# The last layer normalization of a decoder layer in one VectorE pass, its shift as a product in PSUM

## What is computed

```python
def layer_norm(x, g, b):
    xf = x.astype(F32)
    mu = jnp.mean(xf, -1, keepdims=True)
    var = jnp.mean(jnp.square(xf - mu), -1, keepdims=True)
    return ((xf - mu) * lax.rsqrt(var + LN_EPS) * g.astype(F32) + b.astype(F32)).astype(x.dtype)
...
    h = layer_norm(DN_ALPHA * x + mixed, ln1_g, ln1_b)
    f, fbuf = conv_ffn(h, ffn_buf, ffn_w_up, ffn_conv_w, ffn_w_down)
    y = layer_norm(DN_ALPHA * h + f, ln2_g, ln2_b)
```

## Time and profile before

| | us |
|---|---|
| median of 3 runs | 2952.71 |
| lowest, highest | 2946.45, 2958.77 |
| span of the profiled execution | 2947.1 |

### The profile page before, as it was taken

One profiled execution on the slowest core, in us unless ns is written; L12 is line 12 of the kernel. 1 busy time (PEld: TensorE's weight loads), 2 busy tenths in 40 slices (PEclk: granted clock), 3 DMA queues, 4 the chain that ended last, 5 costly groups with the idle time before them and its releaser, 6 DMA issues.

```text
span 2947.1 us, 55566 instructions
## 1 busy us (share of the span) xinstructions
PE 2788.9 (95%) x22685; PEld 2676.0 (91%) x22685; DVE 2278.0 (77%) x3537; ACT 1384.8 (47%) x2371; POOL 359.2 (12%) x332
## 2 busy tenths in 40 slices
PE   8999999999989969999889999999999999999996
PEld 8999999988888658889889999999999999999996
DVE  6656877877657777755688888888888888878898
ACT  4434545545646544522264444444444453434344
POOL 0010000013370315223330000000000000000002
PEclk9999999999989989999999999999999999999998
DMA  7564444448722884563344444444343464434343
GB/s 221 179 206 107 117 119 128 113 150 286 275 82 105 343 247 117 148 175 92 90 157 136 119 126 117 137 115 132 111 141 111 137 194 163 153 112 155 114 124 118
DMA packets 521474, 440.14 MB, mean 149 GB/s; under 512 B 36264, under 2 KB 476767, under 8 KB 515147
## 3 DMA queue, kind: packets, MB, share of 16 engines
q1 hardware_dynamic: 456662, 300.70, 35.6%
q0 software_dynamic: 20288, 82.91, 7.6%
q10 hardware_dynamic: 44272, 52.98, 5.3%
HBM read 378.31 MB, written 66.55 MB: 151 GB/s over the span
## 4 chain that ended last, share of the span: by engine, by line
PE 49%; DVE 5%; issue 1%; ACT 1%; POOL 1%; DMA 1%; DVEq 0%; ACTq 0%; POOLq 0%
PE i L3363 42%; PE i L140 7%; DVE f_half L3869 1%; DMA x_blocks<-s_blk 1%; POOL x_blocks L3311 1%; DVE x_blocks L3907 1%; DVE h_rows L3902 0%; DVE y_rows L4000 0%; DVE w_ring L3858 0%; DVE x_blocks L3835 0%; PE i L3372 0%; DVE y_rows L3993 0%; DVE f_sum L3862 0%; DVE ln_parts L3913 0%; ACT x_blocks L3657 0%
## 5 line engine op out<-in xcount | busy, mean ns | idle before, releaser
L3363 PE MATMUL i<-x_blocks,f_half 128*128 128x272 f32 x10752 | 1357.0, 288 | 26.0 <-DVE h_rows L3902 10.9
L3363 PEld LDWEIGHTS i<-x_blocks,f_half 128*128 128x128 f32 x10752 | 1347.0, 189 | 31.7 <-DVE x_blocks L3907 14.1
L570 PE MATMUL a<-xb_in,w_half 128*128 128x272 f32 x4200 | 546.9, 291 | 8.9 <-DVE w_half L972 4.6
L570 PEld LDWEIGHTS a<-xb_in,w_half 128*128 128x128 f32 x4200 | 536.0, 190 | 18.2 <-issue 7.2
L3586 ACT CAST f_half<-w_ring 128x1024 fp32r<-128x1024 f32 (+2 forms) x370 | 346.2, 936 | 403.1 <-PE i L3363 339.5
L3869 DVE TENSOR_TENSOR f_half<-w_ring,f_half 128x1024 fp32r<-128x1024 f32 (+2 forms) x362 | 393.4, 1087 | 80.3 <-ACT f_half L3586 77.9
L3869 DVE TENSOR_TENSOR f_half<-f_sum,f_half 128x1024 fp32r<-128x1024 f32 (+2 forms) x148 | 159.5, 1078 | 81.4 <-ACT f_half L3586 81.4
L972 DVE TENSOR_TENSOR w_half<-w_ring,w_half 128x1024 fp32r<-128x1024 f32 x129 | 157.5, 1222 | 82.9 <-ACT w_half L708 82.5
L3586 ACT CAST f_half<-f_sum 128x1024 fp32r<-128x1024 f32 (+2 forms) x148 | 138.8, 938 | 150.1 <-PE i L3363 148.9
L3323 POOL TENSOR_TENSOR f_half<-w_ring,f_half 128x512 fp32r<-128x512 f32 x8 | 12.9, 1611 | 1397.0 <-ACT f_half L3586 1397.0
L708 ACT CAST w_half<-w_ring 128x1024 fp32r<-128x1024 f32 x125 | 131.3, 1050 | 108.9 <-PE a L570 104.8
(11 more groups left out here) (576 smaller groups left out, 4170.3 us busy)
## 6 DMA issues: line engine op xcount, KB each, us to landing
w_ring<-in_ffn_w_up_dram SPq DMA_DIRECT2D x88, 1024.0 KB, 6.9
w_ring<-in_w_in_dram SPq DMA_DIRECT2D x52, 1024.0 KB, 8.8
w_ring<-in_ffn_w_down_dram SPq DMA_DIRECT2D x24, 1536.0 KB, 7.9
w_ring<-in_w_o_dram SPq DMA_DIRECT2D x16, 1024.0 KB, 6.1
x_blocks<-s_blk ACTq DMA_DIRECT2D x17, 816.0 KB, 5.9
s_proj<-st ACTq DMA_DIRECT2D x48, 272.0 KB, 2.7
s_blk<-x_sums ACTq DMA_DIRECT2D x22, 544.0 KB, 6.7
kv_ring<-in_cmp_w_dram SPq DMA_DIRECT2D x16, 512.0 KB, 8.1
```

Source lines behind the costliest of these rows:

```text
L570: last = nc.tensor.matmul(ps[bank][:, 0:HT2], half(q, w)[:, k], XB[v[j]][:, k], start=j in (0, 1, 3) and k == 0 and i == 0, stop=k == HK - ...
L3363: last = nc.tensor.matmul(ps[bank][:, 0:HT2], half(e, j, wl_)[:, s], XB[:, x0 + s, xl_, BLK_OF[j]], start=start and s == 0 and i == 0, sto ...
```

## The change

The second normalization is taken in another order: first y is multiplied by gamma, and then one VectorE pass gives (y * gamma) * (1/deviation) + shift, where the shift, (-mean/deviation) * gamma + beta, is a matrix product of a 6-row factor (1 and -mean/deviation, in high and low halves) with six rows of beta and gamma in halves.

- The product with gamma, of 128-column blocks over the four prompt tiles: GpSimd takes two blocks an instruction, one instruction in each of the pairs 2 to 7 of the last chunk and one behind them; VectorE takes the last two blocks (`times_g`).
- The loads of gamma and beta move into the last chunk, behind the 28th weight load of 32. Two loads of one row each follow two pairs later. GpSimd makes from them a rounded copy and its remainder in pair 6, and SyncE copies these to rows 2 to 5 of `BG`.
- VectorE builds the columns of the factor (`SH_T`), TensorE turns them, ScalarE copies them to `SH`. TensorE then makes 16 products of 6x128 by 6x512 into banks 0 to 5, and VectorE makes 16 passes, one for each quarter of each prompt tile.
- ScalarE's copies of gamma and beta into PSUM go. ScalarE and GpSimd keep only the two halves of the sample rows.
- Row 15 is turned into banks 0 and 1, without a wait for the copy of row 14.
- In the last pair VectorE aggregates the first ten rows of statistics of each tile and writes the result back as one entry of `BS`; the last aggregation reads that and six more. The statistics of rows 12 and 13 come one slot and one row earlier.

```diff
+            BG_RAW = at("ln2_bg_raw", [2, DM], F32, h_at)
+            BG_LO = at("ln2_bg_lo", [2, DM], F32R, h_at)
+            BG = at("ln2_bg", [6, DM], F32R, h_at + 4 * row)
+            SH_T = at("ln2_shift_t", [P, QT, 6], F32, s_at + 224)
+            SH_HI = at("ln2_shift_hi", [P, QT], F32R, s_at + 320)
+            SH = at("ln2_shift_rows", [6, QT * P], F32R, x_at + 3 * KT * P * 4 + 1920)
...
-            P_UNITS = [(QT, 0), (QT - 1, 1), (QT, 1)]
+            P_XG, E_ROWS = KT - 2, 10
+            def turn_bank(m):
+                return 6 if m < KT - 1 else 0
...
+                    if g == 3 * HK + 3:
+                        sp.wait_ge(xq, 28)
+                        sp.wait_ge(tout, 32 * (FT // 4))
+                        sp.dma_start(GROW, A["ln2_g"].partition_broadcast(P)[:, 0, :]).then_inc(gr_in, 16)
+                        sp.dma_start(BROW, A["ln2_b"].partition_broadcast(P)[:, 0, :]).then_inc(gr_in, 16)
+                    if g == 3 * HK + 5:
+                        sp.wait_ge(tr, 6)
+                        sp.dma_start(BG_RAW[0:1], A["ln2_b"]).then_inc(bg_in, 16)
+                        sp.dma_start(BG_RAW[1:2], A["ln2_g"]).then_inc(bg_in, 16)
...
-                done = 0
-                for group in V_GROUPS:
-                    t = group[0][0]
-                    for k in range(0, len(group), 2):
-                        done += 2
-                        cols = slice(group[k][1] * Q4, (group[k + 1][1] + 1) * Q4)
-                        sp.wait_ge(yr, done)
-                        sp.dma_start(O[0][0, t * P:(t + 1) * P, cols], YN[:, t, cols]).then_inc(y_out, 16)
-                sp.wait_ge(y_out, 16 * (done // 2))
-                sp.wait_ge(yp_out, YO0 + 16 * len(P_UNITS))
+                sp.wait_ge(bg_lo, BL0 + 1)
+                sp.dma_start(BG[2:4, :].bitcast(F32), BG_LO[:, :].bitcast(F32)).then_inc(bg_rows, 16)
+                sp.dma_start(BG[4:6, :].bitcast(F32), BG[0:2, :].bitcast(F32)).then_inc(bg_rows, 16)
+                for t in range(QT):
+                    for h in range(2):
+                        sp.wait_ge(yr, 4 * t + 2 * h + 2)
+                        sp.dma_start(O[0][0, t * P:(t + 1) * P, half_cols(h)], YN[:, t, half_cols(h)]).then_inc(y_out, 16)
...
+                def times_g(m):
+                    cols = slice(m * P, (m + 2) * P)
+                    gp.wait_ge(bst, m + 2)
+                    g = GROW[:, cols].rearrange("p (o n) -> p o n", o=1).broadcast_to((P, QT, 2 * P))
+                    nc.gpsimd.tensor_tensor(YN[:, 0:QT, cols], YN[:, 0:QT, cols], g, ALU.mult).then_inc(xg, 1)
                 for e in range(NP):
                     for j in range(7):
                         if on_pool(e, j):
                             gp.wait_ge(hq, 7 * e + j + 1)
                             nc.gpsimd.tensor_tensor(half(e, j, 1), source(e, j), half(e, j, 0).bitcast(F32), ALU.subtract).then_inc(lp, 1)
-                gp.wait_ge(gr_in, 32)
-                for k, (t, h) in enumerate(P_UNITS):
-                    r, cols = P if t < QT else NS, half_cols(h)
-                    y = YN[0:r, t, cols]
-                    gp.wait_ge(nz, NZ0 + k + 1)
-                    nc.gpsimd.tensor_tensor(y, y, GROW[0:r, cols], ALU.mult).then_inc(yp, 1)
-                    gp.wait_ge(yp, YP0 + 2 * k + 1)
-                    nc.gpsimd.tensor_tensor(y, y, BROW[0:r, cols], ALU.add).then_inc(yp, 1)
-                    gp.wait_ge(yp, YP0 + 2 * k + 2)
-                    if t < QT:
-                        gp.dma_start(O[0][0, t * P:(t + 1) * P, cols], y).then_inc(yp_out, 16)
-                    else:
-                        gp.dma_start(O[1].rearrange("b t d -> (b t) d")[:, cols], y).then_inc(yp_out, 16)
+                    i = e - NU - 3 * HK
+                    if i == 2:
+                        gp.wait_ge(gr_in, 32)
+                    if i >= 2:
+                        times_g(2 * (i - 2))
+                    if i == 6:
+                        gp.wait_ge(bg_in, BI0 + 32)
+                        gp.wait_ge(tr, 10)
+                        nc.gpsimd.tensor_copy(BG[0:2, :], BG_RAW[:, :]).then_inc(bg_hi, 1)
+                        gp.wait_ge(bg_hi, BH0 + 1)
+                        nc.gpsimd.tensor_tensor(BG_LO[:, :], BG_RAW[:, :], BG[0:2, :].bitcast(F32), ALU.subtract).then_inc(bg_lo, 1)
+                times_g(KT - 4)
...
-                    if m:
+                    if m and m < KT - 1:
                         pe.wait_ge(cp, m)
+                    b = turn_bank(m)
                     for tt in range(QT):
-                        nc.tensor.transpose(ps[6][:, tt * P:(tt + 1) * P], ht(m)[:, tt * P:(tt + 1) * P], ident)
-                    nc.tensor.transpose(ps[7][0:NS, 0:P], ht(m)[:, SEQ:TOK], ident).then_inc(tr, 1)
+                        nc.tensor.transpose(ps[b][:, tt * P:(tt + 1) * P], ht(m)[:, tt * P:(tt + 1) * P], ident)
+                    nc.tensor.transpose(ps[b + 1][0:NS, 0:P], ht(m)[:, SEQ:TOK], ident).then_inc(tr, 1)
...
+                pe.wait_ge(cp, KT - 1)
+                pe.wait_ge(sh, SH0 + 1)
+                for t in range(QT):
+                    last = nc.tensor.transpose(ps[6][0:6, t * P:(t + 1) * P], SH_T[:, t, :], ident)
+                last.then_inc(sh_t, 1)
+                pe.wait_ge(cp, KT)
+                pe.wait_ge(bg_rows, BR0 + 32)
+                pe.wait_ge(sh_r, SR0 + 1)
+                for u in range(4 * QT):
+                    t, q = u // 4, u % 4
+                    if u >= 6:
+                        pe.wait_ge(yr, u - 5)
+                    nc.tensor.matmul(ps[u % 6][:, :], SH[:, t * P:(t + 1) * P], BG[:, q * Q4:(q + 1) * Q4], start=True, stop=True).then_inc(cs, 1)
...
-                act.wait_ge(ed, 7 * 4 * HK)
-                act.wait_ge(gr_in, 32)
-                for q in range(4):
-                    nc.scalar.copy(ps[q][:, :], GROW[:, q * Q4:(q + 1) * Q4]).then_inc(gp_s, 1)
                 act.wait_ge(bst, KT + 1)
-                nc.scalar.activation(RD[:, QT - 1:], MV[:, QT - 1:, 1], ACT.Sqrt, bias=EPS[:, 0:1]).then_inc(dev, 1)
-                act.wait_ge(bst, KT + 2)
-                nc.scalar.activation(RD[:, 0:QT - 1], MV[:, 0:QT - 1, 1], ACT.Sqrt, bias=EPS[:, 0:1]).then_inc(dev, 1)
+                nc.scalar.activation(RD[:], MV[:, :, 1], ACT.Sqrt, bias=EPS[:, 0:1]).then_inc(dev, 1)
+                act.wait_ge(sh_t, ST0 + 1)
+                nc.scalar.copy(SH[:, :], ps[6][0:6, :]).then_inc(sh_r, 1)
...
+                def early_moments(first, to):
+                    for tt in range(first, to):
+                        r = P if tt < QT else NS
+                        last = nc.vector.bn_aggr(MV[0:r, tt], BS[0:r, tt, 0:E_ROWS])
+                    link.link(last)
+                def early_tuples():
+                    n = float(E_ROWS * P // 2)
+                    for k in (0, 3):
+                        nc.vector.memset(BS[:, :, E_ROWS - 1, k:k + 1], n)
+                        nc.vector.tensor_copy(BS[:, :, E_ROWS - 1, k + 1:k + 2], MV[:, :, 0:1])
+                        nc.vector.tensor_scalar(BS[:, :, E_ROWS - 1, k + 2:k + 3], MV[:, :, 1:2], n, None, ALU.mult)
...
-                        if c == 3 and i and n == 6:
+                        if c == 3 and i and n == (6 if more else 5):
                             parts(2 * (i - 1))
+                        if not more and n == 6:
+                            parts(KT - 3)
+                        if not more and n in (2, 3, 4):
+                            early_moments(2 * (n - 2), min(2 * (n - 2) + 2, QT + 1))
+                        if not more and n == 4:
+                            early_tuples()
                 add_down(NP - 1, 6)
-                for m in range(KT - 3, KT):
+                for m in range(KT - 2, KT):
                     parts(m)
                 dve.wait_ge(bst, KT)
-                for first, to in ((QT - 1, QT + 1), (0, QT - 1)):
-                    for tt in range(first, to):
-                        r = P if tt < QT else NS
-                        last = nc.vector.bn_aggr(MV[0:r, tt], BS[0:r, tt])
-                    last.then_inc(bst, 1)
+                for tt in range(QT + 1):
+                    r = P if tt < QT else NS
+                    parts_ = BS[0:r, tt].rearrange("p m s -> p (m s)")[:, (E_ROWS - 1) * 6:KT * 6]
+                    last = nc.vector.bn_aggr(MV[0:r, tt], parts_)
+                last.then_inc(bst, 1)
+                def times_g(m):
+                    cols = slice(m * P, (m + 1) * P)
+                    g = GROW[:, cols].rearrange("p (o n) -> p o n", o=1).broadcast_to((P, QT, P))
+                    nc.vector.tensor_tensor(YN[:, 0:QT, cols], YN[:, 0:QT, cols], g, ALU.mult).then_inc(xg, 1)
+                dve.wait_ge(gr_in, 32)
+                times_g(P_XG)
                 dve.wait_ge(dev, 2)
-                link.link(nc.vector.reciprocal(RD[:, QT - 1:], RD[:, QT - 1:]))
```

(31 more changed lines are left out.)

37 lines of the change are left out of this document (22 added, 15 removed).

## The result

The changed kernel takes 2961.99 us, the median of six runs (2953.67 to 2964.46); the kernel before, beside it, 2952.32 (2946.45 to 2958.77). The ratio is 1.0028, with a 95% interval of 1.0015 to 1.0041: slower by some 8 us by the ratio (9.7 between the two medians), where 5.7 us faster was forecast, and above the range of 2939 to 2954. The profiled execution took 2957.61 us with a span of 2955.8.

What follows compares the result with a forecast made beforehand. TensorE bounds the pairs, VectorE the tail behind them. Gains 0.6 + 1.05 + 9.55, less 3.5 for the lead-in and 0.3 for GpSimd's chain, took 5.7 us off the median: 2947.0 us, range 2939 to 2954.

Steps and rivals of the forecast that it cites:

- Part 1: Behind the pairs: last row's transposes go to a free PSUM bank, so its statistics skip a 0.59 us wait; gain 0.6 us.
- Part 2: Last five aggregations read 42 instead of 96 numbers, 0.264 us each; gain 1.05 us, added work in the last pair free.
- Part 3: In the pairs: GpSimd's products with gamma, the beta/gamma preparation in pair 6 and the moved loads are hidden; no cost.
- rival (b): In the pairs: new GpSimd work stretches VectorE 1.4 us a pair and so slows TensorE; 2955.4 us, chance 0.05.
- Rival (c): Beta/gamma preparation in pair 6 comes late and the last pair stalls; 0.5 to 1.5 us given back, 2948, chance 0.10.
- Part 4: Lead-in from last aggregation to first pass: a chain across engines takes 4.1 us in place of 0.57.
- Part 5: Tail: 16 VectorE passes in place of 28, 0.658 us each; span ends 3.0 us behind the last, at 2941.1.
- Part 6: What ends last: GpSimd's sample-row chain, its last transfer landing in 2.3 us; span ends at 2941.4, 0.3 behind VectorE's path.
- rival (a): Tail: the output transfers become the bound; gain only 3.2 us, time 2949.5 us, chance 0.08.
- share at 1.0 for more than 2 us behind the last pass: Tail: sign that would show the forecast wrong, the transfers' share staying full that long after VectorE's last pass.

Runs made afterwards that it cites:

- e_before_parts12: Kernel before, plus only the free PSUM bank for the last row's transposes and the two-step aggregation; one run, 2951.17 us.
- e_no_sample_out: Changed kernel with beta/gamma preparation over 32 partitions, gamma products re-placed, first output transfer split, and the sample rows' output transfers removed; one run, 2944.19 us.
- e_fit_tuples: Changed kernel, preparation over 32 partitions moved to pair 7, gamma products re-placed and partly VectorE's, pair 7's behind the tiny aggregation operations; 2949.23 us, ratio 0.9984.
- e_no_gamma: Changed kernel with beta/gamma preparation over 32 partitions and GpSimd's seven products with gamma left out; one run, 2945.98 us.

## Why the prediction was wrong, point by point

**Part 1, right.** The last row's statistics follow without a wait, and the last transposes wait for no copy.

**Part 2, right, a little better than forecast.** 1.15/5 = 0.23 us for 42 numbers, 0.264 forecast. Together with part 1 the gain of e_before_parts12 was 1.87 us, 1.65 forecast, and the steps from half to half did not grow.

**Part 3, wrong: this is the step that failed.** It priced GpSimd's new work at nothing because GpSimd had room (4.8 of 12 us), and asked only when GpSimd would be done. Its products cost 3.6 us up to the half of pair 7, 0.6 to 0.7 in most pairs and 1.5 in one step, and the preparation cost 7.6 us in pair 6. Together with what they cost behind that half it is 12.1 us that the step had put at nothing. The price "no cost" rested on the sentence under rival (b) that the sum at L3862 "always begins under GpSimd's half" and stays at 0.672 us. The starts refute it: in the last pair of before

```profile
2908.62 0.67 DVE L3862 TENSOR_TENSOR f_sum<-w_ring 128x512 f32<-128x512 f32 x1
2908.85 1.60 POOL L3323 TENSOR_TENSOR f_half<-w_ring,f_half 128x512 fp32r<-128x512 f32 x1 [10.35 <-ACT f_half L3586]
```

the sum begins 0.23 us ahead of GpSimd's half. It was not VectorE that ran undisturbed under GpSimd; GpSimd waited for VectorE, and its 1.60 us are the 1.29 that the same half takes with no sum beside it, and that wait. "It is GpSimd that stretches" had the right row and read it the wrong way: no VectorE instruction with two SBUF inputs began under a GpSimd one there, so the row could not speak of that case. The stretched 1.60 was itself a mark of the exclusion. The step also mis-added its own upper bound: a remainder stretched by 1.60/1.10 adds 2.1 us, which puts the end of the half at 2913.2 and not 2912.2.

**Rival (b) was the case**, given 0.05: new GpSimd work slows VectorE, and through it TensorE. It had a stretching where the runs show exclusion. It put 1.4 us on each pair; VectorE did lose 1.5 in a pair, but its idle time left 0.6 to 0.7 of it in most pairs, and one pair lost 7.6 us that it had not seen. Its forecast of 2.7 us above before was too small for that reason. Rival (c) had the right place, the preparation in pair 6, and the wrong mechanism: 0.5 to 1.5 us of GpSimd being late, where 7.6 came of VectorE being held. GpSimd was not late: it had idled 7.98 us ahead of its half of pair 7.

**Part 4, right.** From the last aggregation's end at 2936.20 (2935.05 + 1.15) to the first pass at 2940.37: 4.2 us, 4.1 forecast. TensorE had idled since 2933.09, and its granted clock is 0.50 in the windows from 2937.0 on; the four transposes take 1.01 and ScalarE's copy 0.57.

**Part 5, right.** 10.62 us for sixteen passes: 15 x 0.658 + 0.74 = 10.61 forecast.

**Part 6, mis-sized by 1.5 us.** GpSimd's chain lasted as forecast, 10.77 us from 2940.57 to 2951.34. But its last transfer needs 3.9 us to land and not 2.3, and the span ends 4.8 us behind the last pass and not 3.0, or 3.3 with GpSimd's chain. The step took both landings over from a tail in which 28 passes fed the queues; with 16 the queues fill. This is rival (a), given 0.08: its sign "share at 1.0 for more than 2 us behind the last pass" is there. It put the gain at 3.2 us for 5.7, 2.5 less; measured were 1.5 less. It also reckoned with 4.32 MB where 4.46 are sent. e_no_sample_out shows what tips it: without the sample rows' 0.26 MB the end is back at 3.07. The 393 to 406 GB/s in the two windows behind the last pass are of the size of the 418 of the earlier trace rows; these rows do not agree with the limit of about 358 GB/s a core that rival (a) takes from the Trainium skill (DMA: Bandwidth & Descriptors, section Where 436 GB/s comes from).

The sum on the after side: 6.1 us gained from the first pass on, 2.4 lost ahead of it behind TensorE's end, 11.2 lost ahead of that; 7.6 us slower. The 11.2 are 12.1 of collision less the 0.9 that part 1 brings forward (TensorE ends 82.76 us behind the half of pair 2; with e_before_parts12's last pair it would be 59.67 + 11.01 = 70.68). Without the collision the gain is 4.3 us, as e_fit_tuples and e_no_gamma show; the forecast said 5.7. The rest, 1.4, is of the size of part 6's 1.5.

## What to carry to other kernels

A free engine is not free memory access. Before work goes to GpSimd, list what VectorE runs in that stretch: sums, copies and scalings from SBUF to SBUF are held for the whole of each GpSimd instruction, whatever its width in partitions, and then everything queued behind them; statistics and forms with an input in PSUM are not. So keep GpSimd's instructions short, spread over many partitions, and start each by a wait on the last VectorE instruction ahead of a stretch of the free forms. And when a row is taken as evidence that two engines don't disturb each other, compare the starts and the ends: which of the two began under the other, and which of them was stretched. Starts within some 0.2 us of each other do not say which was held.

## What the runs showed of the hardware

- VectorE and GpSimd take turns on SBUF by whole instructions: 0.69 us become 2.33 under a 2.34 us product, 1.79 under a 1.89 us copy, 2.25 under a product of 2 partitions; five elements a partition 0.16 become 2.10. Statistics and forms with an input in PSUM keep their length.
- The same holds for GpSimd behind VectorE: 1.29 us for 512 elements become 1.60 behind one sum and 2.53 behind two operations.
- A GpSimd instruction costs by its length along the free dimension: 2x2048 takes 4.35 us (4.82 with its wait), 32x128, the same count of numbers, 0.88 with its wait; a product of 2x1024 takes 2.33, of 128x1024 2.34.
- Aggregation costs by the count of its numbers: 0.474 us for 96, 0.35 for 60, 0.23 for 42.
- Two transfers of 128 KB from 32 partitions cost the stream of outputs 1.7 us when GpSimd issued them, and the end came no earlier when ScalarE did (15.92 us behind the first pass for 15.43). Around the first of them the engines' share is 0.96 at 201 GB/s; transfers of 512 KB from 128 partitions move at about 390 to 410 GB/s.
